# Squares of queries and keys issued on ScalarE before, instead of behind, the copy of a value block's projection

## The reference, cut to what matters

```python
qkv = jax.nn.silu(_dwconv(qkv, p['gdn_conv_w']))     # 1536 columns, 4 taps along the tokens
q, k, v = jnp.split(qkv, 3, axis=-1)
q = _l2norm(heads(q, GDN_H)) * GDN_DK ** -0.5        # 4 heads of 128
k = _l2norm(heads(k, GDN_H))
# _l2norm(x) = x * rsqrt(sum(x * x, axis=-1) + EPS)
```

## Time and profile before

| what | value |
|---|---|
| median of 3 runs | 1076.65 us |
| lowest and highest run | 1075.4 and 1076.88 us |
| profiled execution, span from its first to its last instruction | 1071.6 us |
| runs' median less that span | 5.05 us |
| PE busy | 942.1 us, 88% |
| VectorE busy | 443.8 us, 41% |
| ScalarE busy | 257.5 us, 24% |
| mean granted clock of PE | 0.956 |

### The profile page before, as it was taken

The page is one execution under the profiler, slowest core; times in us unless marked ns, Lnnn a source line. Parts: engine busy times, 40 slices in busy tenths (PEclk is TensorE's granted clock), DMA queues, the critical chain, the costliest instruction groups (busy, mean ns, idle before and its releaser), DMA issues.

```text
span 1071.6 us, 23772 instructions
## 1 busy us (share of the span) xinstructions
PE 942.1 (88%) x10749; PEld 655.2 (61%) x10749; DVE 443.8 (41%) x734; ACT 257.5 (24%) x436; POOL 134.6 (13%) x154
## 2 busy tenths in 40 slices
PE   2799998878999889999999799998899999999940
PEld 2554576765665446688999664565858756665510
DVE  1443767974345333465667631555100010100037
ACT  3418233233113227231322310220101101100103
POOL 4000000000003100554246000001000000000021
PEclk9899999989999999999999989988999999999985
DMA  8902008654021900200000247142589999999845
GB/s 297 382 27 79 1 1 316 238 175 147 8 78 61 339 19 1 83 19 22 2 3 23 78 179 313 60 177 94 211 304 386 398 403 383 398 394 395 347 156 195
DMA packets 55772, 192.60 MB, mean 180 GB/s; under 512 B 7323, under 2 KB 10834, under 8 KB 51570
## 3 DMA queue, kind: packets, MB, share of 16 engines
q1 hardware_dynamic: 42096, 161.09, 39.7%
q0 software_dynamic: 6736, 22.81, 6.6%
q10 hardware_dynamic: 6834, 7.11, 1.9%
HBM read 168.27 MB, written 22.73 MB: 178 GB/s over the span
## 4 chain that ended last, share of the span: by engine, by line
PE 74%; DVE 11%; DMA 6%; ACT 4%; issue 4%; ACTq 1%; DVEq 0%; SPq 0%; POOLq 0%
PE ps L731 16%; PE ps L1199 14%; PE ps L1222 7%; PE ps L1019 6%; PE ps L1072 6%; PE ps L721 4%; PE ps L1007 4%; PE ps L976 3%; DMA ring<-in_moe_w_up 2%; PE ps L870 2%; PE ps L821 2%; PE ps L748 2%; DMA ring<-in_ada_w 1%; PE ps L1140 1%; PE ps L967 1%
## 5 line engine op out<-in xcount | busy, mean ns | idle before, releaser
L731 PE MATMUL ps<-hT,ring 128*128 128x128 f32 x704 | 194.2, 437 | 1.9 <-ACT hT L1323 1.9
L731 PEld LDWEIGHTS ps<-hT,ring 128*128 128x128 f32 x704 | 106.8, 193 | 83.6 <-issue 80.1
L2440 DVE TENSOR_TENSOR hT<-ps,hT 128x384 f32<-128x384 f32 (+3 forms) x18 | 9.1, 506 | 245.9 <-ACT hT L1641 235.7
L1199 PE MATMUL ps<-ring,arena 128*32 128x128 f32 (+3 forms) x1104 | 87.3, 377 | 2.5 <-DMA ring<-in_moe_w_up 1.3
L1199 PEld LDWEIGHTS ps<-ring,arena 128*32 128x32 f32 (+1 forms) x1104 | 61.1, 118 | 28.5 <-issue 20.4
L1796 POOL DMA_INDIRECT arena<-h_rows,slot_tok x18 | 16.6, 922 | 384.4 <-PE ps L721 229.5
L1199 PE MATMUL ps<-arena 128*32 128x256 f32 (+2 forms) x1056 | 60.8, 387 | 4.4 <-DVE arena L2432 2.7
L1199 PEld LDWEIGHTS ps<-arena 128*32 128x32 f32 x1056 | 46.7, 112 | 19.4 <-issue 5.0
L721 PE MATMUL ps<-ident,arena 128*128 128x128 f32 (+3 forms) x316 | 44.3, 289 | 11.6 <-DVE arena L2207 5.0
L721 PEld LDWEIGHTS ps<-ident,arena 128*128 128x128 f32 (+3 forms) x316 | 39.3, 177 | 20.6 <-issue 7.7
L2178 DVE TENSOR_TENSOR arena<-arena,ps 128x512 f32<-128x512 f32 x50 | 34.4, 688 | 29.5 <-PE ps L1019 28.7
(11 more groups left out here) (438 smaller groups left out, 1485.3 us busy)
## 6 DMA issues: line engine op xcount, KB each, us to landing
ring<-in_ada_w SPq DMA_DIRECT2D x12, 2048.0 KB, 11.3
ring<-in_moe_w_gate SPq DMA_DIRECT2D x7, 2048.0 KB, 9.9
arena<-in_moe_w_gate SPq DMA_DIRECT2D x7, 2048.0 KB, 10.7
arena<-in_moe_w_up SPq DMA_DIRECT2D x7, 2048.0 KB, 15.6
arena<-in_moe_w_down SPq DMA_DIRECT2D x7, 2048.0 KB, 20.4
ring<-in_moe_w_up SPq DMA_DIRECT2D x7, 2048.0 KB, 16.5
ring<-in_moe_w_down SPq DMA_DIRECT2D x7, 2048.0 KB, 21.9
ring<-in_w_in SPq DMA_DIRECT2D x6, 2048.0 KB, 12.8
```

The costliest lines, as they stand in the source:

```text
L731: last = mm(out, w[:, k, cols], rhs(k)[:, a:b], start=(k == 0), stop=(k == KD - 1))
L1199: last = mm(ps[rows_of(n, g), GU, 512 * i + at:512 * i + at + width], m_xgT[:, b % 2, k, rows_of(n, j)], w[:, k, col:col + width], start=( ...
```

## The change

On ScalarE the two squares of a value block go ahead of the copy of that block's projection. Each now waits for the SiLU of its own input. The squares' slots are turned by one: square n lies in slot (n + 1) % 4, under a name of its own (`a_sqs`, at the same place in SBUF), and so it is the fourth square (n = 3) that takes the slot of `a_abT` and waits for the transposes. PE reads the squares from the new slots.

```diff
+        a_sqs = carve(5120, 4, T)
...
-                        last = mm(out, ones[:, :], a_K.rearrange("p a b -> p (a b)")
-                                  .rearrange("p (n t) -> p n t", t=T)[:, n % 4, a:e], start=True, stop=True)
+                        last = mm(out, ones[:, :], a_sqs[:, (n + 1) % 4, a:e], start=True, stop=True)
...
-            sqs = a_K.rearrange("p a b -> p (a b)").rearrange("p (n t) -> p n t", t=T)
             narrow("ab", a_abT)
             act.wait_ge(s_a_pad, 3)
             for b in range(8, 12):
+                for n in (2 * b - 16, 2 * b - 15):
+                    act.wait_ge(s_a_silu, 2 * n + 2)
+                    if n == 3:
+                        act.wait_ge(*full_after(("abT", 0)))
+                    if n >= 4:
+                        act.wait_ge(*full_after(("ss", n - 4)))
+                    A(a_sqs[:, (n + 1) % 4, :], a_qk[:, n, :], ACT.Square).then_inc(s_a_sq, 1)
                 qkv(b)
                 silu_out(b - 1)
-                if b == 8:
-                    act.wait_ge(*full_after(("abT", 0)))
-                    act.wait_ge(s_a_silu, 16)
-                for n in (2 * b - 16, 2 * b - 15):
-                    if n >= 4:
-                        act.wait_ge(*full_after(("ss", n - 4)))
-                    A(sqs[:, n % 4, :], a_qk[:, n, :], ACT.Square).then_inc(s_a_sq, 1)
             silu_out(11)
```

## The result

| | before | after |
|---|---|---|
| first comparison, median of 4 runs each | 1076.77 us | 1063.92 us |
| profiled execution, span | 1071.6 us | 1063.1 us |
| its own time | not listed | 1064.8 us |

The ratio is 0.987, with a 95% interval of 0.9825 to 0.9915. On the 1076.65 us of the forecast that is 1062.7 us, between 1057.8 and 1067.5. The forecast, 1065.5, is a ratio of 0.9897 and lies within the interval; but the range began at 1063.0, 0.3 us above 1062.7. The kernel gained more than was forecast: 12.9 us between the medians, 14.0 by the ratio, where 11.1 stood. Runs of the kernel before that took over 1.5% longer than the fastest of their batch, four of the 80 on record, don't count in the ratios and means of this text.

The account below looks back on a forecast made before the run. TensorE (PE) was taken to bound the kernel, waiting four times for ScalarE's squares. Blocks 9 to 11 give 7.08 us, block 8 4.03 (2.34 gap, 1.69 clock): 1076.65 - 11.11 = 1065.5 us, range 1063 to 1069 us.

Parts of the forecast that it names:

- The mechanism: Blocks 8 to 11: squares ahead of the copy remove PE's four waits; 4.03 us plus 7.08 us, chance 0.60.
- ScalarE's chain: Logs and exponentials before PE's cumulative sums: slack shrinks from 4.96 to 2.60 us; rival that PE waits, 1067.9 us, chance 0.07.
- The rival of a new wait in ScalarE's queue: From the fifth square, waiting for the sum four before could hold a projection's copy; slower, 1081.5 us, chance 0.03.
- the PSUM pairs: Sums might wait for a PSUM pair to be emptied; seven us left at block 10's second sum; all gain gone, 1076.6 us.
- the clock term of block 8: Block 8's sums ran at 0.59 of full clock behind the gap; without it 1.00 expected, worth 1.69 us, called uncertain.
- the rival with two falls: Timed runs of before lose the clock twice (3.38 us) where the profile shows one; gain 12.8 us, 1063.9 us, chance 0.05.
- a clock not given back: Block 8's clock loss stays, or wasn't in the timed runs; gain 9.42 us, 1067.2 us, chance 0.20.
- the range's lower end: 1063 us: the first four cases lie between 1063.9 and 1067.9 us, with about 1 added at both ends.
- The span and the median: Profiled span 1071.6 us, runs' median 1076.65 us; the 5.05 us between them left as is, the gain taken off the median.

Follow-up runs that it names:

- filled gaps: Kernel before, order of squares kept, with eight extra matmul records on PE in each of the four gaps ahead of the sums; ratio 0.9951 (0.9917 to 0.9984).
- the other edits: Only block 8's squares ahead (ratio 1.000), only later pairs ahead (0.9934), gaps with eight extra matmul records (0.9951) or four (single run), block 6's SiLU moved (0.9868, 0.9848).
- the second edit: Changed kernel with the SiLU of block 6 also moved behind the five HGRN2 copies; ratios to the kernel before 0.9868 and 0.9848, mean 1061.7 us.

## Why the prediction was right, and where it was wrong

**The mechanism was right, step by step.** PE's four waits for the squares were waits of the kernel. With the squares ahead they are gone, no other wait took their place, and all of the stage's 11.3 us (against a trace of before with one fall) arrives at the first load behind it. Block by block: block 8 gives 15.32 - 11.40 = 3.92 us (4.03 forecast), each of the others 13.28 - 10.82 = 2.46 us (2.36 forecast). The 0.1 us more come from the sums, which take 2.33 instead of 2.43 us when they follow a projection without a pause.

**ScalarE's chain didn't become the wait**: its slack is 2.49 us. The rival of a new wait in ScalarE's queue had no part in it, nor did the PSUM pairs: PE has no idle time ahead of any sum.

**The step that failed is the clock term of block 8**, "I take one, since that is the one execution I see". The term was mis-sized: one fall, 1.69 us, stood in the sum, and eight traces have 11 falls, 1.4 for each, or 2.3 us. The filled gaps show that the term is real. That it is a matter of the execution was in the text, and the rival with two falls gave 1063.9 us; what was wrong was to take the one execution for the middle, and to lean the chances the other way, 0.20 for a clock not given back and 0.05 for two falls: each of the eight traces has a fall, three have two. With the measured figures the sum is 11.9 us, 1064.7 us on the same median. So of the 2.8 us between 1065.5 and 1062.7 the falls account for 0.6 and the shorter sums for 0.2; the other 2 us are within the first comparison's uncertainty, about 4.8 us either way.

**The second failing, and the larger one, is the range's lower end**, "the runs of before differ by 1.5 us, so I add about 1 at both ends". 76 runs lie 18 us apart. Drawing three at random from these, their median falls between 1072.5 and 1082.3 us nine times in ten, so a forecast that starts from a median of three carries some 5 us either way, whatever is known of the change. A measurement of this kernel can tell about 0.45% from no change, as the first comparison's interval shows (four runs against four), and not 0.2%.

**The span and the median** were put 5.05 us apart "which I leave as it is". All later runs have 1.7 to 1.9 us there. So by my estimate the profiled execution of before took some 1073.4 us, 3.3 less than the median beside it: a short execution, and not the middle of the runs that it was taken for.

**What stays open.** The timed gain is 13.2 us with a 95% interval of about 1.5 either way, and the stage gives 11.9. The rest, 1.3 us, lies within the uncertainty, and no run settles where it is if it is real. The table of traces has one candidate: the expert loads take 256.2 us on the average of eight traces of before and 254.0 in three of after. But the chunks of the DeltaNet go the other way (164.0 and 167.0), and both stretches vary within one kernel by up to 5 us. Also, the expert loads took 252.4 to 255.2 us in the six traces of the other edits, whether their stage was short or, with filled gaps, 53.47 us; this speaks against the order of the squares as the cause. Where the filled gaps gain 3.4 us beyond their stage is open as well. Their 12 runs have a mean granted clock of 0.956, those of before 0.952, but no trace shows in which stage. Why the 16 runs of the changed kernel lie closer together (2.3 us) than those of before (4.3) and of the kernel with the second edit (5.2) wasn't settled either.

## What to carry to other kernels

Where the chain of waits runs through an engine that does several small things per step in order, look for work whose input has been there for long but which stands behind a copy that waits for the bottleneck: putting it into the engine's idle time gives back the whole wait, and costs nothing as long as the moved work doesn't itself wait for that step. Price a gap on TensorE as its idle time, plus the lost overlap of about 0.17 us, plus the clock behind it, which a single trace shows for that execution only. Before a range is given, look at how a run's time varies; the distance between the span of the profile and the median of the runs is a first hint.

## What the runs showed of the hardware that wasn't expected

The same idle time of TensorE costs the clock in some executions and not in others. Behind the gap of block 8, two short transposes and 2.2 us of nothing, the granted clock fell in all eight traces of before; behind the three other gaps of the same length in three of 24 cases. In the windows shown it was 0.58 to 0.59 over some 4 us, and each fall cost about 1.7 us. The one trace with block 8's gap at 1.96 us has the fall too, and behind the gap of 2.06 us ahead of the narrow projection it fell in three of the 15 traces that have this gap. When the gap of block 8 alone was taken away, the one trace had a fall at block 10; whether it moved there or would have come anyway isn't shown. Over a whole run a lower granted clock goes with a longer time: a run of the kernel before with a mean of 0.947 took 1083.08 us, one with 0.960 took 1069.51 us, and over its 72 runs with a listed clock the correlation is -0.89. How much of that is falls behind gaps like these wasn't traced.
